# Four output copies moved to a later place in GpSimd's DMA queue of a hybrid decoder step

## The reference

```
h = rmsnorm(x, norm_g);  z = h @ w_in                     # 3332 columns, four mixers
k_att, v_a, logf, shift = parts of z                       # are outputs as well
o_a = attention over q, k, v with forget gates             # 4 heads x 64; prompt and paged cache
o_b = rwkv7 recurrence;  o_c = causal pooling;  o_d = conformer convolution
x = x + concat(o_a*silu(g_a), o_b*silu(g_b), o_c*silu(g_c), o_d*silu(g_d)) @ w_out
y = rmsnorm(x, final_norm_g)
# outputs: y, and per layer k, v, logf, the rwkv state, the last rows for shift, pool and conv
```

## Time and profile before

| | us |
|---|---|
| median of 3 runs | 1790.43 |
| lowest, highest | 1788.74, 1791.56 |
| the profiled execution | 1791.56 |
| its span, first to last instruction | 1789.7 |

### The profile page before, as it was taken

How to read it: one execution, slowest core, us unless ns; L and a number is a source line. 1 busy time by engine, 2 the same in 40 slices (tenths; PEclk the granted TensorE clock), 3 DMA queues, 4 the chain that set the end, 5 groups by cost and what they waited for, 6 DMA issues and landing times.

```text
span 1789.7 us, 34734 instructions
## 1 busy us (share of the span) xinstructions
PE 1694.2 (95%) x14646; PEld 1019.0 (57%) x14646; DVE 787.7 (44%) x1678; ACT 472.5 (26%) x850; POOL 117.8 (7%) x166
## 2 busy tenths in 40 slices
PE   6999999999999999999899999899999869999997
PEld 3555555555555455587456555688887644444442
DVE  5450499942121335321676655355555451212111
ACT  5301100001052623101456545322222440000000
POOL 1100000021100000000000000000000001121110
PEclk9999999999999999999899999999999989999998
DMA  6324322175613145820744554766552577898872
GB/s 246 107 84 143 104 85 72 36 232 161 167 60 132 36 190 203 291 82 33 228 146 137 151 155 151 238 202 192 172 174 80 199 282 252 285 313 281 317 275 77
DMA packets 150421, 302.88 MB, mean 169 GB/s; under 512 B 16661, under 2 KB 120933, under 8 KB 131894
## 3 DMA queue, kind: packets, MB, share of 16 engines
q1 hardware_dynamic: 128330, 155.52, 27.8%
q0 software_dynamic: 17280, 117.18, 19.1%
q10 hardware_dynamic: 4656, 27.96, 3.8%
HBM read 237.75 MB, written 65.10 MB: 169 GB/s over the span
## 4 chain that ended last, share of the span: by engine, by line
PE 75%; DVE 13%; ACT 4%; issue 3%; DMA 3%; SPq 2%; ACTq 0%; DVEq 0%
PE psum L817 27%; PE psum L1072 14%; PE psum L1362 14%; DVE big L1774 8%; PE psum L1035 4%; PE psum L898 3%; PE psum L788 3%; PE psum L993 3%; PE psum L1018 2%; SPq L559 2%; PE psum L843 2%; ACT big L1432 1%; DMA big<-in_aux 1%; PE psum L1335 1%; PE psum L885 1%
## 5 line engine op out<-in xcount | busy, mean ns | idle before, releaser
L817 PE MATMUL psum<-big,wbuf 128*128 128x416 f32 x1920 | 677.3, 514 | 12.7 <-DVE big L1680 11.4
L817 PEld LDWEIGHTS psum<-big,wbuf 128*128 128x128 f32 x1920 | 365.4, 191 | 319.2 <-issue 314.3
L1072 PE MATMUL psum<-big 64*64 64x64 f32 (+2 forms) x5792 | 212.1, 259 | 19.9 <-issue 11.0
L1072 PEld LDWEIGHTS psum<-big 64*64 64x64 f32 (+1 forms) x5792 | 165.1, 132 | 76.1 <-issue 48.1
L1405 ACT ACTIVATE zst<-psum 128x416 f32<-128x416 f32 x123 | 63.1, 517 | 534.2 <-PE psum L817 534.1
L1362 PE MATMUL psum<-big 128*128 128x512 f32 (+1 forms) x408 | 189.0, 614 | 8.6 <-issue 8.6
L1774 DVE SCALAR_TENSOR_TENSOR big<-big,pars 128x2048 f32<-128x2048 f32 x120 | 148.2, 1298 | 1.1
L1362 PEld LDWEIGHTS psum<-big 128*128 128x128 f32 (+1 forms) x408 | 74.3, 189 | 106.3 <-issue 106.3
L2218 DVE TENSOR_TENSOR zst<-zst,psum 128x1024 f32<-128x1024 f32 (+1 forms) x17 | 20.8, 1221 | 234.3 <-PE psum L1362 234.3
L688 POOL DMA_INDIRECT big<-in_cache_v,pidx x64 | 60.6, 947 | 797.0 <-PE psum L1035 509.6
L1663 ACT ACTIVATE big<-zst 128x1024 f32<-128x1024 f32 (+1 forms) x17 | 18.0, 1057 | 297.0 <-DVE zst L2218 297.0
(11 more groups left out here) (246 smaller groups left out, 1673.2 us busy)
## 6 DMA issues: line engine op xcount, KB each, us to landing
big<-in_k_pages SPq DMA_DIRECT2D x432, 128.0 KB, 2.3
zT<-zst ACTq DMA_DIRECT2D x25, 1040.0 KB, 6.5
wbuf<-in_w_slots SPq DMA_DIRECT2D x24, 512.0 KB, 4.5
big<-zT POOLq DMA_DIRECT2D x11, 1024.0 KB, 5.5
zst<-in_k_pages SPq DMA_DIRECT2D x80, 128.0 KB, 2.4
rwS<-big POOLq DMA_DIRECT2D x8, 1024.0 KB, 4.2
big<-rwS SPq DMA_DIRECT2D x8, 1024.0 KB, 5.7
zst<-in_x_prompt SPq DMA_DIRECT2D x16, 512.0 KB, 8.7
```

What stands on the lines that cost most here:

```text
L817: last = nc.tensor.matmul(psum[:, m % CHUNKS, 0:CW], w[:, k, :], x, start=(k == 0), stop=(k == KT - 1))
L1072: return nc.tensor.matmul(out, l, r, start=start, stop=stop, skip_group_check=True)
```

## The change

Only POOL's list changes. Before, the two `kT` copies and `shiftE` are issued in the second round of the loop that stores the recurrence's operands, between the `rkk` store and the four `rwS` stores. After, they are gone from there. `kT` is issued when `o_read` has reached 12, right ahead of `vE` and `logfE`, and `shiftE` right behind them. `vE` and `logfE` waited for `o_read` 5 and are now behind the wait for `o_read` 12 too. The waits for the stores of slots KA and KA+1 go; the new place is past them.

```
--- before.py
+++ after.py
@@ -754,11 +754,6 @@
                 pool.wait_ge(rkk_ready, t + 1)
                 pool.dma_start(rkk[t], rw_t[:, :]).then_inc(rkk_stored, 16)
-                if t == 1:
-                    for x in range(2):
-                        z_ready(KA + x)
-                        pool.dma_start(O['kT'][x], zT[KA + x]).then_inc(st_stored, 16)
-                    pool.dma_start(O['shiftE'], zT[R0:R0 + 7, :, SEQ - 1:T_ALL]).then_inc(st_stored, 16)
                 for n, (m, src) in enumerate(((1, rw_kk), (0, rw_r), (2, rw_k), (3, rate[:, t]))):
@@ -769,11 +764,14 @@
             pool.wait_ge(idx_ready, 1)
             cv = I['cache_v'].rearrange("n l (r j) h d -> (n l r) (j h d)", r=RT)
+            pool.wait_ge(o_read, 12)
+            for t in range(2):
+                pool.dma_start(O['kT'][t], zT[KA + t]).then_inc(st_stored, 16)
             pool.wait_ge(vf_evac, TT + 1)
-            pool.wait_ge(o_read, 5)
             pool.dma_start(O['vE'], vtok[:, :, 0:256]).then_inc(st_stored, 16)
             pool.wait_ge(nl_ready, 2)
             pool.dma_start(O['logfE'], lo).then_inc(st_stored, 16)
+            pool.dma_start(O['shiftE'], zT[R0:R0 + 7, :, SEQ - 1:T_ALL]).then_inc(st_stored, 16)
             pool.wait_ge(sc_mm, KSTEPS)
```

## The result

| | us |
|---|---|
| before, median of 4 runs (lowest, highest) | 1789.59 (1786.02, 1791.56) |
| after, median of 4 runs (lowest, highest) | 1810.10 (1802.24, 1813.62) |
| ratio of the times, 95% interval | 1.0114 [1.0085, 1.0144] |
| after, the profiled execution; its span | 1800.94; 1799.2 |

The change makes the kernel slower, by 20 us in this first comparison. The forecast was slower by 12.5 us, and the measured median lies 4 us above the range. In two later comparisons on other chips the same kernel gave 1.0068 [1.0042, 1.0093] and 1.0063 [1.0041, 1.0085], 13 and 12 us. The profiled execution is not one of the four in the table and is faster than all of them: 9.4 us above the profiled execution of before, which is the slowest of its four. So the profile has to explain 9 us, and the experiments have to say what the other runs have.

What follows compares the result with a forecast made beforehand. TensorE's projection matmuls bound the old place, a tight page-load/key-step pair the new; 0 + 0 + 10.8 (wait) + 1.7 (clock) = +12.5 us on the 1790.4 median gives 1802.9 us, range 1792.5 to 1806.

Steps and rivals of the forecast that it cites:

- The tight pair: SP's 16 page loads land at 930.6 us, TensorE's key step needing them starts at 931.12: slack about 0.5 us.
- The removal at 687 and at 886: Clearing copies from 687 us gives at most 2.0 us, from 886 us at most 0.5; both taken as 0.
- rival 3: At the key step behind item 13 no stall appears, only relief remains: −2.5 us at best, −1.5 likely; chance 0.09.
- The order of the queues: From 924.4 us DMA engines alternate packets; the copies' queue needs fewer turns than the pages' 82, so pages end last.
- Rival 1: Engines split time by bytes: key step behind item 13 waits about 2 us, +3 us in all; chance 0.14.
- Rival 2: Several page pieces go per turn: key step behind item 13 waits 5.4 us, +7 us in all; chance 0.14.
- The new waiting: TensorE's key step behind item 13 starts at 941.9 us instead of 931.12, waiting for pages: 10.8 us.
- The term for q0: From 924.4 us the moved copies in POOL's queue occupy each DMA engine alone for 12.9 us.
- so 82 are 3.7 us: At 924.4 us 1320 page packets remain in SP's queue, 82 per engine, taking 3.7 us.
- The clock: After the idle time at about 931 us TensorE's matmuls run slower: 1.7 us, bounds 0 and 2.7.
- Given back: After the stalled key step, later attention steps neither stall again nor catch up; later SP and POOL waits cost 0.
- Rival 4: The next step's pages also meet the tail of the copies: another 2 to 3 us, 1805.5 us; chance 0.08.

Runs made afterwards that it cites:

- e9: Kernel before, with only the two kT copies moved: SP issues them in its own queue behind the 16 page loads for the key step behind item 13; 0.9996 of before.
- e6: Kernel before, with kT and shiftE issued behind the recurrence's last page loads, before the gathers; vE and logfE stay at o_read 5; 1.0024 of before.
- e2: Kernel before, with only the two kT copies moved to o_read 12; shiftE, vE and logfE stay; 1.0055 of before.
- e3: Kernel before, with only the wait of vE and logfE raised from o_read 5 to 12; kT and shiftE stay; 1.0069 of before.
- e7: Changed kernel with all five copies released at o_read 13 in place of 12; 1.0057 of before.
- e8: Changed kernel with all five copies released at o_read 10 in place of 12; 1.0039 of before.
- e1: The changed kernel run again unaltered on another chip, for a second profile; 1.0068 of before, profiled execution 1817.01 us.
- e5: The kernel before run again unaltered, to see how far two profiles of one program drift; 0.9992 of before.

## Why the prediction was wrong

**What bounds the kernel, and the place of the loss: right.** The tight pair of page loads and key step behind item 13, the release at about 923.5 (measured 923.24), one stall on the pages there, and none at the next step are as forecast.

**The removal at 687 and at 886: right as far as the traces show.** I took 0. The `rwS` stores did not move. TensorE's idle time before the sample step, 1.98 us before, is 1.82, 1.98 and 2.25 us in the three profiles of the change, and its busy time in 886 to 898 us is 11.54 us before and after. e9, which takes only `kT` away, is at 0.9996. No relief of 2.0 us shows; rival 3 is out. e6, which takes `shiftE` away too, is 0.1 to 0.4% slower, and why is open.

**The order of the queues: right.** 414 packets to 418, and e2 and e3 with 6.4 and 6.2 us, bear out that the pages end last. Rival 1 (a wait of 2 us) and rival 2 (5.4 us) are refuted by the 12.95 us. The Trainium skill (DMA: Bandwidth & Descriptors, queues, rings and completion order) says that an engine takes its queues in turn, a packet of typically 9 to 17 descriptors at a time. The trace agrees that they take turns. Turns of so many page rows of 1 KB against single packets of 4 KB of `vE` would not give 414 to 418; turns of equal length on both sides would, and the counts can't tell these from single packets.

**The new waiting, 10.8 us: this step failed in size.** It was 12.95, 15.03 and 13.05 us in three profiles. The term for q0, 12.9 us, was right: 67.3% of 19.2 us is 12.9. The term mis-sized is the one for what q1 still had to carry, "so 82 are 3.7 us", from 1320 packets at 924.4 us. Up to the key step q1 carried 1983 packets in 5.7 us, which is about 2.0 of the 2.15 us that the sum lacks. The count had two holes. The DMA view of the profile after, 919 to 948 us, holds just the 16 pages and four 64 KB transfers of SP:

```profile
q1 hardware_dynamic: 2880, 2.36, 29.3%
```

That is 20 x 144, so a page is 144 packets and not 128. And I left out the four transfers (lines 523 and 530 before), which SP issued behind the pages from 929.28 us on. The engines worked them off in the same time; why that came before the last page row was through, the views don't show, since they don't tell the 16 engines apart. In e7 and e8 the sum came 4 us too short with the engines 100% and 98% busy, so q1's work was too small there as well.

**The clock, 1.7 us: right.** 3.64 for 1.93 us, 1.71 more. The first matmuls behind it run at the lower level too, and the chain is 14.6 us late at the next key step, where my terms gave 12.5.

**Given back: partly wrong.** I said nothing is given back. In the first profile 1.4 us come back by the end of the attention (14.6 to 13.2), and 3.7 more later. The waits at later key steps don't explain the first (5.4 us in three before, 5.7 in five after), but the clock behind them does: before, two key steps took 3.58 and 2.87 us in place of 1.93, after only one, 2.94. The second is not repeated in e1, so it is no property of the change.

**The base and the range: what made the interval miss.** With the wait as it was, 12.95 us, the sum would have given 1805.1 us, still inside the range; some 5 us lie elsewhere. I set 12.5 us on a median of 1790.43 and gave 3.2 us of room above 1802.9. The after kernel has medians of 1810.10, 1811.05 and 1807.52 in three comparisons, nearly steady, while before has 1789.59, 1797.84 and 1795.05. So the size of the effect that three comparisons share is 12 to 14 us, near the forecast, and the first one shows 20. Why before was low and the change high in it is not settled: the only profile of the change from that comparison is of its fastest execution, which shows 9.4 us. The drifts of 5 to 16 us between profiles of one program (e1, e5) are large enough for it. A range that knew only three runs of before, within 3 us of each other, had no right to be that narrow above.

**Rival 4, a second stall: refuted.** The key step behind item 15 waits 0 in all three profiles of the change.

## What to carry to other kernels

A transfer that nobody waits for is not free: look up which loads with a deadline are in flight when it is released, and what slack they have (here 0.5 us). In this trace the two queues sent equal numbers of packets, of 4 KB and of at most 1 KB, and the small ones finished last. Issue such a copy behind the urgent loads, as e9 did in their own queue, or where the trace shows no deadline. And count everything that the loads' own queue has to carry by the deadline, not the loads alone: that was the term that came out too small here. Small loads count as well: with the release moved away from the pages, a 64 KB tile became the thing that was late. And take the width of a forecast from how far the same program drifts between chips and clock levels, not from three runs.

## What the runs showed of the hardware

- A copy from DRAM to DRAM of 2.1 MB delays loads from DRAM to SBUF by as much as a 2.2 MB store from SBUF does: 6.4 and 6.2 us (e2, e3).
- Cutting 33 KB packets to 4 KB changed the delay of the other queue by 0.05 us (6.39, 6.34).
- With both queues backlogged the 16 DMA engines were 97, 98 and 100% busy (after, e8, e7). A page load of 128 KB shows as 144 packets, of which 128 are rows of 1 KB.
- SP's own issue took longer while its queue was backed up. The 16 page loads took 8.43 us to issue before and up to 12.60 (e3). Two gate tiles that took 0.42 us each to issue before took 3.30 and 2.88 us in the profile after, in SP's timeline:

```profile
929.84 3.30 SPq L523 DMA_DIRECT2D pars<-zT  x1
...
934.74 2.88 SPq L523 DMA_DIRECT2D pars<-zT  x1
```

For these two it cost nothing here, since SP had nothing urgent behind them.
